# Second operand block of the down projection's second product in the weight buffers, two loads ahead of the last store, and squares ahead of roots

## What is computed

```python
h2 = rms_norm(x, n2_pre) * (1 + sc2) + sh2
up = depthwise_conv(h2 @ ffn_w_up, fdw_w, fdw_b)
a, gl = jnp.split(up, 2, axis=-1)
x = x + g2 * rms_norm((jax.nn.silu(a) * gl) @ ffn_w_down, n2_post)
```

## Time and profile before

| what | value |
|---|---|
| median of 3 runs | 2146.61 us (2145.95 to 2146.74) |
| the profiled execution, its own time | 2144.68 us |
| its span in the profile | 2142.7 us |
| PE busy | 2084.1 us (97%) |
| DVE, ACT, POOL busy | 1684.9, 828.1 and 964.3 us |
| mean granted TensorE clock | 0.991 |

### The profile page before, as it was taken

How to read it: one execution, slowest core, us unless ns; L and a number is a source line. 1 busy time by engine, 2 the same in 40 slices (tenths; PEclk the granted TensorE clock), 3 DMA queues, 4 the chain that set the end, 5 groups by cost and what they waited for, 6 DMA issues and landing times.

```text
span 2142.7 us, 30746 instructions
## 1 busy us (share of the span) xinstructions
PE 2084.1 (97%) x12055; PEld 1882.1 (88%) x12055; DVE 1684.9 (79%) x1906; ACT 828.1 (39%) x1378; POOL 964.3 (45%) x597
## 2 busy tenths in 40 slices
PE   7999999999999999999999999999999999988998
PEld 3887887887887999999999988999999999967886
DVE  3699899899899587787447536799998988866867
ACT  3512212212222466656448233343333333433344
POOL 1445645546545466666372121146666656650000
PEclk9999999999999999999999999999999999999999
DMA  9442432432422545544654344222222322346452
GB/s 305 127 142 84 140 127 95 132 123 98 135 90 95 195 151 172 173 142 142 233 166 150 130 157 141 89 62 62 79 77 62 93 62 79 123 160 242 159 183 107
DMA packets 233760, 283.08 MB, mean 132 GB/s; under 512 B 11441, under 2 KB 176145, under 8 KB 233617
## 3 DMA queue, kind: packets, MB, share of 16 engines
q1 hardware_dynamic: 180785, 212.41, 31.3%
q10 hardware_dynamic: 51424, 63.98, 9.0%
q0 software_dynamic: 1408, 4.72, 0.6%
HBM read 214.06 MB, written 67.01 MB: 131 GB/s over the span
## 4 chain that ended last, share of the span: by engine, by line
PE 81%; DVE 10%; DMA 3%; ACT 2%; issue 2%; SPq 1%; POOL 1%; ACTq 0%; DVEq 0%; POOLq 0%
PE ps L1120 80%; DVE conv_y L2579 2%; DVE f_cv L2914 1%; DVE T_raw L2869 1%; DMA A_raw<-g_d 1%; PE ps L1335 1%; SPq L764 1%; DVE Al L2953 1%; DMA x_all<-in_x_sample 1%; DVE T_lo L2895 1%; DMA r_raw<-rT_d 0%; PE ps L1383 0%; DVE T_r L2994 0%; DVE Bl L2959 0%; DVE x2t L3052 0%
## 5 line engine op out<-in xcount | busy, mean ns | idle before, releaser
L2579 DVE SCALAR_TENSOR_TENSOR conv_y<-u_in,VC,conv_y 128x1167 f32<-128x1167 f32 x240 | 482.2, 2010 | 9.6 <-ACT conv_y L1749 2.6
L1120 PE MATMUL ps<-A_hi,Wa_hi 128*128 128x384 f32 x768 | 260.9, 340 | 0.5 <-DVE A_lo L2536 0.5
L1120 PE MATMUL ps<-A_hi,Wa_lo 128*128 128x384 f32 x768 | 258.1, 336 | 0.0
L1120 PE MATMUL ps<-A_lo,Wa_hi 128*128 128x384 f32 x768 | 258.0, 336 | 0.0
L2281 POOL TENSOR_TENSOR Wa_lo<-W_raw,Wa_hi 128x1024 fp32r<-128x1024 f32 x58 | 156.5, 2705 | 223.2 <-ACT Wa_hi L1627 223.0
L2914 DVE SCALAR_TENSOR_TENSOR f_cv<-f_in,VF,f_cv 128x1023 f32<-128x1023 f32 (+1 forms) x176 | 213.0, 1260 | 1.8
L2433 POOL TENSOR_TENSOR O_lo<-E,O_hi 128x512 fp32r<-128x512 f32 x80 | 130.4, 1631 | 152.4 <-ACT O_hi L1627 152.4
L2433 POOL TENSOR_TENSOR O_lo<-F_raw,O_hi 128x512 fp32r<-128x512 f32 x68 | 112.2, 1651 | 145.2 <-ACT O_hi L1627 145.2
L1120 PE MATMUL ps<-Wb_hi,A_lo 128*128 128x512 f32 x432 | 169.3, 392 | 0.0
L1120 PE MATMUL ps<-Wb_hi,A_hi 128*128 128x512 f32 x432 | 169.1, 391 | 0.0
L1120 PE MATMUL ps<-Wb_lo,A_hi 128*128 128x512 f32 x432 | 168.7, 391 | 0.0
(11 more groups left out here) (338 smaller groups left out, 5525.5 us busy)
## 6 DMA issues: line engine op xcount, KB each, us to landing
F_raw<-in_ffn_w_up SPq DMA_DIRECT2D x44, 512.0 KB, 6.1
qt<-qkvg_d SPq DMA_DIRECT2D x36, 512.0 KB, 3.6
W_raw<-in_w_in SPq DMA_DIRECT2D x32, 512.0 KB, 4.7
W_raw<-in_w_in SPq DMA_DIRECT2D x64, 256.0 KB, 3.1
ada_w<-in_ada_w ACTq DMA_DIRECT2D x30, 512.0 KB, 3.9
F_raw<-in_ffn_w_down SPq DMA_DIRECT2D x30, 512.0 KB, 5.2
A_raw<-g_d SPq DMA_DIRECT2D x30, 512.0 KB, 3.8
g_d<-f_cv SPq DMA_DIRECT2D x22, 576.0 KB, 3.6
```

What stands on the lines that cost most here:

```text
L1120: return pe.matmul(out, l, r, start=start, stop=stop)
L2579: dve.scalar_tensor_tensor(out=y, in0=x, scalar=tap, in1=y, op0=ALU.mult, op1=ALU.add).then_inc(q.conv_step, 1)
```

## The change

Four things are done, and the rest of the diff renumbers semaphores for them.

1. M_5's second activation block of each step (`kh` = 1) is loaded to `F_raw` by `b_load` instead of to `A_raw` by `a_load`. In M_5 each of the two kinds of buffer then holds one tile a step, four steps deep. The first two of these loads wait for the buffers of M_1's step 4 (`sum_last(4)` on DVE, `low_x(4)` on POOL), the next two for those of step 5, the last two for `sum_first` of M_5's own steps 0 and 1, and all of them for the last store.
2. The weight loads 8 and 9 (M_1's step 4) are issued ahead of the last store `g_store(21)` instead of behind it. They wait for `sum_last(2)`, since they use the buffers of step 2.
3. DVE's `low_a(2)` comes ahead of `side_taps(FKT - 1, 1)` instead of behind it.
4. At the end, ACT does the squares of the tiles 8, 0, 1, 2, 3 in one row and then their roots, all at step 38, instead of square and root in turns, three tiles at step 38 and two behind the copies of step 39. DVE scales all five at step 38, followed by `finish(8)` and `finish(0)` there, `finish(1)` at step 39, `finish(2)` at step 40 and `finish(3)` behind `scaled(4, 0)`; stores of the tiles follow that order.

```diff
--- before.py
+++ after.py
@@ -574,10 +574,11 @@
             return PAIR_BANK[(2 * p + h) % 3]
         CTX_BANK = 4
 
-        A_FROM = [(M_1, i, 0, 0) for i in range(6)] + [(M_5, i, 1, kh) for i in range(6) for kh in range(2)]
+        A_FROM = [(M_1, i, 0, 0) for i in range(6)] + [(M_5, i, 1, 0) for i in range(6)]
         A_FROM += [(M_7, i, 1, 1) for i in range(6)] + [(M_3, i, 0, 1) for i in range(6)]
         A_FROM += [(M_2, i, 0, 1) for i in range(6)] + [(M_4, i, 1, 1) for i in range(6)]
-        B_FROM = [(M_1, i, 0, ch) for i in range(6) for ch in range(2)] + [(M_6, i, 1, 1) for i in range(6)]
+        B_FROM = [(M_1, i, 0, ch) for i in range(6) for ch in range(2)] + [(M_5, i, 1, 1) for i in range(6)]
+        B_FROM += [(M_6, i, 1, 1) for i in range(6)]
         B_FROM += [(M_7, i, 0, 0) for i in range(6)] + [(M_3, i, 1, 1) for i in range(6)] + [(M_2, i, 1, 0) for i in range(6)]
         def a_no(p, i, n=0):
 
@@ -636,7 +637,8 @@
             n = X_ORDER.index(t)
             return xt_in[n % 2], XT_LAST[n % 2] + 16 * (n // 2 + 1)
         SQUARES = [(t, 1) for t in (4, 5, 6, 7, 8, 0, 1, 2, 3)]
-        for t_ in (8, 0, 1, 2, 3, 4, 5, 6, 7):
+        SQUARES += [(t, 0) for t in (8, 0, 1, 2, 3)] + [(t, "root") for t in (8, 0, 1, 2, 3)]
+        for t_ in (4, 5, 6, 7):
             SQUARES += [(t_, 0), (t_, "root")]
         def e_no(t, what):
 
@@ -645,7 +647,7 @@
         def z_no(t, half):
 
             return Z_0 + Z_ORDER.index((t, half)) + 1
-        OUT_ORDER = [(8, 0), (0, 0), (1, 0), (2, 0), (4, 0), (4, 1), (3, 0), (5, 0), (5, 1), (6, 0), (6, 1), (7, 0), (7, 1)]
+        OUT_ORDER = [(8, 0), (0, 0), (1, 0), (2, 0), (3, 0), (4, 0), (4, 1), (5, 0), (5, 1), (6, 0), (6, 1), (7, 0), (7, 1)]
         def o_no(t, half=0):
 
             return OUT_ORDER.index((t, half)) + 1
@@ -1007,16 +1009,22 @@
                         sp.wait_ge(q.d_sb, sb_no(p_, i_))
                     if p_ == M_1:
                         sp.wait_ge(q.w_lo, N_LM + N_OP + 2 * i_ + 2)
+                    elif p_ == M_5:
+                        sp.wait_ge(q.d_sa, s1_no(i_))
                     elif p_ != M_6:
                         sp.wait_ge(q.d_lb, lo_b_no(6 * p_ + i_))
                 k0, n = PAIRS[i]
-                sp.dma_start(F_raw[b % 4][:, 0:512 * n].rearrange("p (k n) -> p k n", k=n),
-                             wd[:, kh * HK + k0:kh * HK + k0 + n, ch * 512:(ch + 1) * 512]).then_inc(wl_in[b % 4], 16)
+                if p == M_5:
+                    sp.wait_ge(q.g_st, 16 * FKT)
+                    src = g_d[HK + k0:HK + k0 + n, :, 512:1024].rearrange("k p n -> p k n")
+                else:
+                    src = wd[:, kh * HK + k0:kh * HK + k0 + n, ch * 512:(ch + 1) * 512]
+                sp.dma_start(F_raw[b % 4][:, 0:512 * n].rearrange("p (k n) -> p k n", k=n), src).then_inc(wl_in[b % 4], 16)
             def a_load(a):
 
                 p, i, th, kh = A_FROM[a]
                 k0, n = PAIRS[i]
-                dst = a_slot(p, i) if p != M_5 else A_raw[(a - 6) % 4]
+                dst = a_slot(p, i)
                 if a < 6:
                     sp.wait_ge(q.f_ps, product_no(FKT - 1, U_S2 if a == 0 else U_S1 if a < 3 else U_S4))
                 elif a < 10:
@@ -1080,9 +1088,11 @@
             b_load(7)
             a_load(4)
             a_load(5)
+            b_load(8)
+            b_load(9)
             g_store(FKT - 1)
-            for b in range(8, 12):
-                b_load(b)
+            b_load(10)
+            b_load(11)
             def out_store(t):
 
                 sp.wait_ge(q.e_o, o_no(t, 1 if 4 <= t < 8 else 0))
@@ -1105,7 +1115,7 @@
                     x2_load(X_ORDER[s - 13])
                 if 34 <= s < 38:
                     x2_load(X_ORDER[s - 29])
-            for t in (8, 0, 1, 2, 4, 3, 5, 6):
+            for t in (8, 0, 1, 2, 3, 4, 5, 6):
                 out_store(t)
             sp.wait_ge(q.e_o, o_no(7, 0))
             sp.dma_start(out_xs[0, 7 * P:8 * P, 0:512], x2t[7][:, 0:512]).then_inc(q.out_st, 16)
@@ -2260,12 +2270,9 @@
                         square(t, 1)
                 if s == 38:
                     ctx_copy(0)
-                    for t in (8, 0, 1):
+                    for t in (8, 0, 1, 2, 3):
                         square(t, 0)
-                        root(t)
-                if s == 39:
-                    for t in (2, 3):
-                        square(t, 0)
+                    for t in (8, 0, 1, 2, 3):
                         root(t)
             for t in range(4, 8):
                 square(t, 0)
@@ -2966,10 +2973,9 @@
                 p, i = divmod(s, 6)
                 w = wide(s)
                 if p == M_5:
-                    a = a_no(M_5, i)
-                    dve.wait_ge(*a_in(a))
-                    dve.wait_ge(*a_in(a + 1))
-                    r1, r2 = A_raw[(a - 6) % 4][:, 0:w], A_raw[(a - 5) % 4][:, 0:w]
+                    dve.wait_ge(*a_in(a_no(M_5, i)))
+                    dve.wait_ge(*b_in(b_no(M_5, i)))
+                    r1, r2 = a_slot(M_5, i)[:, 0:w], F_raw[b_no(M_5, i) % 4][:, 0:w]
                     dve.tensor_tensor(r1, r1, r2, ALU.add).then_inc(q.d_sa, 1)
                 elif p == M_6:
                     b = b_no(M_6, i)
@@ -3105,8 +3111,8 @@
             sum_last(0)
             sum_last(1)
             low_a(1)
+            low_a(2)
             side_taps(FKT - 1, 1)
-            low_a(2)
             side_taps(FKT - 1, 0)
             sum_last(2)
 
@@ -3134,21 +3140,20 @@
                     for t in (8, 0, 1) if s == 35 else (2, 3):
                         scaled(t, 1)
                 if s == 38:
-                    for t in (8, 0, 1, 2):
+                    for t in (8, 0, 1, 2, 3):
                         scaled(t, 0)
-                if s == 39:
                     finish(8)
                     finish(0)
+                if s == 39:
+                    finish(1)
                 if s == 40:
-                    scaled(3, 0)
-                    finish(1)
+                    finish(2)
             last_block(4)
             scaled(4, 0)
-            finish(2)
+            finish(3)
             last_block(5)
             scaled(5, 0)
             finish(4)
-            finish(3)
             last_block(6)
             scaled(6, 0)
             finish(5)
```

## The result

The changed kernel takes 2125.95 us (median of 4 runs, 2123.32 to 2129.53) against 2146.56 (4 runs, 2145.95 to 2146.74): 0.990 of the time, 95% interval 0.9889 to 0.9912, 20.6 us less. 2125.2 was forecast.

What follows compares the result with a forecast made beforehand. PE was busy nearly throughout, so only its idle and half-clock stretches could go: 18.8 us up to M_6 plus 2.6 at the end, 21.4 off 2146.6, gives 2125.2 us; 8-in-10 range 2120.5 to 2132.

Steps and rivals of the forecast that it cites:

- Step 3 of M_1: PE would start this step at 1895.4 instead of 1896.18, after a wait near 1.2 us for low_a(3).
- its 0.8 and 5.1: Gains in M_1: 0.8 us left from moving low_a(2), 5.1 us from PE's shorter wait for Xl.
- Step 4: In M_1, start at 1906.0 behind POOL's low_x(4), PE waiting 2.3 us instead of 7.4; 1904.9 without DVE and POOL taking turns.
- The clock: PE would keep full clock after a 2.3 us wait; both half-clock stretches go, gaining 2.9 and 3.1 us.
- rival A: At M_1's step 4 PE stands 3.2 us and half clock falls once more, costing 3.8 us: 2129; chance 0.15.
- M_5: Runs without a PE stall, sums 5.45 us apart; 6.9 us of waits here and at M_6's start go.
- M_6's start: M_6 would start at 1948.4 instead of 1967.2, a gain of 18.8 us.
- The end: After M_2, reordered squares, roots and finishes gain 2.6 us; step 39's low part 0.2 late, last finish at 2136.0.
- rival C: The end gives nothing: roots and finish(0) ahead of low_a(39) hold PE at step 39; 2127.8, chance 0.06.
- The sum: Whole kernel: 18.8 us up to M_6 plus 2.6 us at the end, 21.4 us together.
- Rival B: M_5 starves in part: loads in flight land in 7 to 8 us; 2128 to 2133, middle 2130, chance 0.12.
- Rival D: M_5's loads don't run ahead; the 9.9 us loop stays, at 11.3: 2154.4; chances 0.03 slower, 0.02 same.

Runs made afterwards that it cites:

- `low_a(2)` behind: The changed kernel with DVE's low_a(2) put back behind the taps: 2123.95 us, 0.9888 of the kernel before.
- the product on DVE: The changed kernel with POOL's last product moved to DVE, behind low_a(3): 2124.8 us, 0.9897 of the kernel before.
- The end only: The kernel before with only the changed order of squares, roots, scaling and finishes at the end: 2144.9 us, 0.9987 of the kernel before.
- second profile: The changed kernel as it is, timed and profiled again beside other kernels on one chip: 2124.5 us, against 2147.5 for the kernel before.
- two deep: The changed kernel with both loads of each M_5 step waiting for the step two before, though buffers are free: 2142.5 us, 0.9975 of the kernel before.

## Why the prediction was right, step by step

Times count from M_1's first matmul (1869.09 before; 1874.14 in the first profile after).

The steps as a whole: what bounded M_5, what would bound step 4 in its place and what the end gives were forecast as they came. The nearness of the median, 0.8 us, is in part luck: it is less than the 3.9 us between two executions of this kernel, and the fall of the clock was left out on a ground that did not hold.

- *Step 3 of M_1* was to start at 26.3 (1895.4); it did at 26.1 (1900.28), with a wait of 1.2 us, as forecast. That 0.8 us of gain would remain from moving `low_a(2)` was wrong in effect: the start of step 4 doesn't depend on it ("`low_a(2)` behind": nothing lost). The sum did not suffer, since its 0.8 and 5.1 are two parts of one gain, step 4's start moved from 1911.9 to 1906.0.
- *Step 4* was to start at 36.9 (1906.0) after a wait of 2.3; it did at 36.7 (1910.83) after 2.1. The working held: the product ends when DVE's string of sums and low parts lets go of it, at 5.74 us, and one turn for `sum_last(4)` falls into `low_b(4)` (3.37), none into `low_x(4)` (2.35). That POOL and DVE take turns is supported by "the product on DVE": the same multiply then takes DVE 1.34 us, and POOL's `low_x(4)` is the one of 3.37, beside a `sum_last(4)` of 3.03. The Trainium skill, SBUF — State Buffer, section "Who interferes with whom", has a DVE instruction with two SBUF inputs contend with a GpSimd instruction that reads SBUF. The trace agrees: 1905.8 at the times of before, against 1906.0 forecast by that rule and 1904.9 without it.
- *The clock* is the step that was only partly right. The prediction took full clock since 2.3 us of wait is nearer to the 2.0 that had no fall than to the 4 that had one, and put a second fall only behind a wait of 3.2 (rival A, 3.8 us). But a fall came behind a wait of 2.1 in one profile of two, and cost 1.6: with it the stretch is 253.6, without it 252.0. "The end only" shows that the reasoning from the length of the wait fails, with falls behind 1.9 and 2.0 us. That full clock came true in three of the four profiles with this wait was luck. The two falls of before were read as 5.7 and 6.3 us of PE's work; the means of 0.56 and 0.79 in the earlier trace rows put their ends at 1917.9 and 1955.4, so 6.0 and 6.1, with the same sum.
- *M_5* has no wait of PE, as forecast. But its sums are 4.54 us apart, not 5.45: DVE runs ahead at its own pace, four operations of 1.14, until it is held by `Ah`'s three buffers at the fifth step. PE never sees this.
- *M_6's start.* Step 9's operands came free at 88.88 before (1957.97), at 72.65 (1946.79) and in the second profile at 71.05 (1941.29 - 1870.24). These are 16.2 and 17.8 less, and 1.2 of wait at M_6's start went as well: 17.4 and 19.0. The forecast was 18.8.
- *The end* was to give 2.6 and gave 2.36. The low part of step 39 was to be 0.2 late and was 0.5: the squares were reckoned 0.81 us apart, but ACT paused 0.4 us ahead of the fourth, and the table load and the roots behind it moved with it.

```profile
2094.85 0.63 ACT L2239 ACTIVATE ej<-y_lo 128x512 f32<-128x512 f32 x1 [0.39 <-ACT ej L2239]
```

These 0.3 us are still there in the low part of step 41 (1.5 earlier, forecast 1.7) and the last reciprocal (2.3, forecast 2.6). There was one table load, as forecast, and PE's waits in M_4 were 1.0 us together. So rival C (the end gives nothing) did not come.
- *The sum*, 21.4, is 21.65 in the profile without a fall and 20.05 in the one with. The medians say 20.6.

How the gain divides: alone, the buffers give 9.6 us of stretch, the loads ahead 4.1, the end 2.3, 16.0 together; all three give 21.7. The 5.6 above the sum are there because step 4 and M_5's loop both hang on POOL's last product and run side by side up to M_6: with either one left, part of what the other saves is waited for again. PE's waits ahead of M_4 show it: 16.1 us before, 10.2 with the buffers only, 14.2 with the loads only, but 3.3 with both, 5.0 less than these two gains would make. Taken from the changed kernel, the depth is worth 17.8, the loads ahead 9.1, the end 2.3, `low_a(2)` nothing.

Rival B (loads in flight late) did not come: the first load for M_5's second block took 4.0 us from issue to DVE's sum, the next sum waited 0.5 us. Rival D's loop of 9.9 us is what "two deep" shows: it needs the wait for two steps before, which the new buffers take away.

Still open: what decides whether the clock falls behind a wait of 2 us, and why PE's waits ahead of M_1 differ between executions of one kernel.

## What to carry to other kernels

When a stage waits for loads at a period well above its compute (9.9 against 5.45 us here), look at what the load's own issue waits for: here a buffer two steps deep made the loop, and idle buffers of another kind, used by no one in that stage, opened it, with the same bytes from the same queue. Two limits that start at one point and are each long enough to hold the next stage were here worth more together than the sum of each alone, so a part that looks small by itself (4.1 us for the loads ahead) can be worth twice that once the other limit is gone (9.1). And when an operation is moved to take away a wait, ask whether the next wait behind it has a cause of its own: `low_a(2)` only moved 0.8 us from one wait to the next.

## What was not expected of the hardware

The granted clock fell after PE was already back at work, 1.4 us behind the end of a wait of 2.1 us, and stayed at 1.2 GHz for 3.4 us; in three other profiles with the same wait it did not fall. In "the end only" it fell behind waits of 1.9 and 2.0 us, and not behind one of 2.4. Behind waits of 7 to 9 us it was low for 5.0 to 6.0 us of PE's work, behind one of 4.5 us for 3.4 us. And POOL's multiply of 2.67 us takes 5.72 to 5.74 beside DVE's back-to-back operations on two tiles from SBUF, in each of the 11 profiles where it is on POOL.
